# The first modulation vectors: five of eight weight pieces summed on TensorE instead of VectorE

## The reference

```python
ada = jax.nn.silu(c) @ w_ada[l] + b_ada[l]          # c: (1, 1024), w_ada[l]: (1024, 6144)
sh1, sc1, g1, sh2, sc2, g2 = [a[:, None, :] for a in jnp.split(ada, 6, axis=-1)]
h = x * (1.0 + sc1) + sh1
...
qa, ka, va, qb, kb, vb = jnp.split(h @ w_in, AB_SPLITS, axis=-1)
```

## Time and profile before

| | |
|---|---|
| median of three runs | 1322.96 us |
| the profiled execution | 1323.02 us, span 1321.2 us |
| TensorE busy | 1236.3 us (94%) |
| VectorE busy | 678.9 us (51%) |
| ScalarE busy | 512.3 us (39%) |
| DMA | 394.99 MB, mean 299 GB/s |
| TensorE busy in the first 20 us | 1.46 us |
| first matmul of weight unit 0 | 20.01 us |
| first matmul of weight unit 4 | 52.65 us |

### The profile page before, as it was taken

How to read it: one execution, slowest core, us unless ns; L and a number is a source line. 1 busy time by engine, 2 the same in 40 slices (tenths; PEclk the granted TensorE clock), 3 DMA queues, 4 the chain that set the end, 5 groups by cost and what they waited for, 6 DMA issues and landing times.

```text
span 1321.2 us, 16525 instructions
## 1 busy us (share of the span) xinstructions
PE 1236.3 (94%) x6620; PEld 856.5 (65%) x6620; DVE 678.9 (51%) x1178; ACT 512.3 (39%) x744; POOL 70.1 (5%) x107
## 2 busy tenths in 40 slices
PE   4898799999999999999999999999999999999977
PEld 2787577788778877788887887444444444544435
DVE  6678868698766777764558566111111111111145
ACT  2646464344464457443445275111111211112135
POOL 0101000000000000001000300000000000000021
PEclk9998899999999999999999999999999999999998
DMA  9988567998555535776555678999999999999960
GB/s 376 373 285 210 206 245 280 270 349 318 213 192 206 193 124 200 262 287 204 197 191 203 205 270 355 381 427 429 429 429 428 369 430 428 429 429 429 428 252 32
DMA packets 43689, 394.99 MB, mean 299 GB/s; under 512 B 5712, under 2 KB 6432, under 8 KB 9712
## 3 DMA queue, kind: packets, MB, share of 16 engines
q1 hardware_dynamic: 33424, 336.63, 64.6%
q0 software_dynamic: 9904, 57.34, 12.9%
q10 hardware_dynamic: 304, 0.23, 0.1%
HBM read 392.50 MB, written 2.46 MB: 299 GB/s over the span
## 4 chain that ended last, share of the span: by engine, by line
PE 60%; DMA 19%; DVE 12%; ACT 5%; issue 3%; SPq 1%; DVEq 0%; ACTq 0%
DMA slabs<-in_w 13%; PE psum L1220 13%; PE psum L676 9%; PE psum L683 9%; PE psum L679 9%; DMA w_raw<-in_units 5%; PE psum L1259 4%; DVE w_parts L1860 3%; ACT w_parts L1330 2%; PE psum L1167 2%; DVE aring L1843 2%; PE psum L949 1%; PE psum L729 1%; PE psum L961 1%; PE psum L1175 1%
## 5 line engine op out<-in xcount | busy, mean ns | idle before, releaser
L1860 DVE TENSOR_TENSOR w_parts<-w_raw,w_parts 128x2048 fp32r<-128x2048 f32 x110 | 251.4, 2289 | 121.4 <-ACT w_parts L1330 121.4
L1330 ACT ACTIVATE w_parts<-w_raw 128x2048 fp32r<-128x2048 f32 x110 | 209.6, 1911 | 121.9 <-DMA w_raw<-in_units 121.8
L1220 PE MATMUL psum<-slabs,arena 128*64 128x512 f32 x1024 | 224.3, 593 | 11.7 <-DMA slabs<-in_w 11.7
L676 PE MATMUL psum<-w_parts,h_parts 128*128 128x512 f32 x448 | 179.8, 401 | 17.3 <-DVE w_parts L1860 13.1
L679 PE MATMUL psum<-w_parts,h_parts 128*128 128x512 f32 x448 | 176.5, 394 | 0.0
L1220 PEld LDWEIGHTS psum<-slabs,arena 128*64 128x64 f32 x1024 | 72.8, 137 | 159.8 <-issue 141.0
L1330 ACT ACTIVATE arena<-psum 128x512 f32<-128x512 f32 (+1 forms) x59 | 33.3, 567 | 281.5 <-PE psum L1232 153.3
L683 PE MATMUL psum<-w_parts,h_parts 128*128 128x512 f32 x448 | 121.5, 394 | 0.0
L676 PEld LDWEIGHTS psum<-w_parts,h_parts 128*128 128x128 f32 x448 | 85.1, 190 | 39.9 <-DVE w_parts L1860 16.3
L683 PEld LDWEIGHTS psum<-w_parts,h_parts 128*128 128x128 f32 x448 | 85.2, 190 | 18.3
L1843 DVE CUSTOM_DVE_ANT_0 aring<-aring,cb 128x1024 f32<-128x1024 f32 x80 | 94.5, 1219 | 3.4 <-DMA aring<-in_ada 3.4
(11 more groups left out here) (306 smaller groups left out, 1769.1 us busy)
## 6 DMA issues: line engine op xcount, KB each, us to landing
slabs<-in_w SPq DMA_DIRECT2D x64, 2048.0 KB, 17.1
w_raw<-in_units SPq DMA_DIRECT2D x110, 1024.0 KB, 5.0
aring<-in_ada POOLq DMA_DIRECT2D x40, 1024.0 KB, 5.2
arena<-in_w SPq DMA_DIRECT2D x16, 2048.0 KB, 17.8
w_odd<-in_w SPq DMA_DIRECT2D x16, 2048.0 KB, 21.2
staged<-in_ada SPq DMA_DIRECT2D x8, 1024.0 KB, 18.3
ln_rows<-in_ln_rows POOLq DMA_DIRECT2D x4, 1024.0 KB, 7.4
slabs<-in_units SPq DMA_DIRECT2D x4, 1024.0 KB, 10.7
```

The lines of the kernel that those rows point to most:

```text
L676: mm(psum[:, bank, :], high(tile, tok), w_hi(k)[:, col:col + 512], start=first and bank not in begun, stop=False, skip_group_check=True)
L1220: ins = nc.tensor.matmul(psum[s * CAP:(s + 1) * CAP, w, :], xe_t[:, kt, s * CAP:(s + 1) * CAP], slab(w, s, b)[:, kt * FE:(kt + 1) * FE], s ...
L1330: return nc.scalar.activation(out_ap, in_ap, func, **kw)
L1860: v.tensor_tensor(w_lo(k), raw(k), w_hi(k).bitcast(F32), ALU.subtract).then_inc(w_split, 1)
```

## The change

Five of the first eight pieces, those at places 0, 1, 3, 5 and 7 (`BY_PE`), are now laid out with 128 inputs on the partitions. TensorE sums them: for each of two halves of 128 outputs, eight matmuls with a 128 x 128 block of the piece as the weights and one column of the activated `c` as the moving operand (`ada_piece`). VectorE only adds the bias to the sums in PSUM. Pieces 2, 4 and 6 stay on VectorE.

- `c` comes as 8 columns of `vec`, which is now the first transfer; ScalarE activates these 8 columns first. The copies `cb` are queued after unit 0 and activated after its high part.
- `x_first` comes in three transfers: tiles 0 and 1 ahead of piece 0, tiles 2 and 3 ahead of piece 2, tiles 4 to 7 ahead of piece 4.
- ScalarE does `first_h(p)` before the high part of unit p, VectorE does `first_low(p)` before the low part.
- TensorE does the 16 matmuls with the high weights of a unit first (L733 and L737 of the new file), for which it waits only for `w_hi_ready`, and the 8 with the low weights last (L744). Products of pieces 0 and 1 come first of all, that of piece 3 after unit 0, those of pieces 5 and 7 between the high and the low matmuls of units 1 and 2.
- GpSimd's first transfer waits for unit 3 instead of piece 7.

```diff
+BY_PE = (0, 1, 3, 5, 7)
...
+        def staged_count(n):
+            return 32 if n in (0, 2, 3, 5) else 16
+        def sums_of(n):
+            i = BY_PE.index(n)
+            return psum[:, 5 + i % 3, 2 * i:2 * i + 2]
...
             def stage(n):
-                sp.dma_start(staged[n][:], a["ada"][ADA_ORDER[n]]).then_inc(staged_in[n], 16)
+                src = a["ada_rows"][BY_PE.index(n)] if n in BY_PE else a["ada"][ADA_ORDER[n]]
+                sp.dma_start(staged[n][:], src).then_inc(staged_in[n], 16)
...
-            sp.dma_start(cb[:], a["c_rows"]).then_inc(silu_c, 16)
-            sp.dma_start(vec[:], a["vecs"]).then_inc(staged_in[0], 16)
+            sp.dma_start(vec[:], a["vecs"]).then_inc(silu_c, 16)
             for i in range(4):
+                if i == 1:
+                    sp.dma_start(cb[:], a["c_rows"]).then_inc(staged_in[2], 16)
+                if i < 3:
+                    tiles = slice(2 * i, 2 * i + 2 if i < 2 else KT)
+                    sp.dma_start(x_first[:, tiles, :], a["x_t"][:, tiles, :]).then_inc(staged_in[(0, 3, 5)[i]], 16)
                 stage(2 * i)
                 stage(2 * i + 1)
...
-            pool.wait_ge(staged_in[STAGED - 1], 16)
+            pool.wait_ge(w_loaded[3], 16)
...
+            def ada_piece(n):
+                pe.wait_ge(staged_in[n], staged_count(n))
+                pe.wait_ge(silu_c, 17)
+                for i in range(2):
+                    for kt in range(KT):
+                        ins = mm(sums_of(n)[:, i:i + 1], staged[n][:, kt * 256 + i * P:kt * 256 + (i + 1) * P],
+                                 V("c", kt), start=kt == 0, stop=kt == KT - 1)
+                ins.then_inc(ada_mm, 1)
+
+            def first_values(i, between=None):
+                k = V_AT + i
+                parts = [(2 * i + s, slice(1024 * s + 512 * c, 1024 * s + 512 * c + 512), c) for s in range(2) for c in range(2)]
+                pe.wait_ge(w_hi_ready, k + 1)
+                for t in range(TT):
...
+                if between is not None:
+                    ada_piece(between)
+                weights(k)
+                for t in range(TT):
...
+            ada_piece(0)
+            ada_piece(1)
...
-                    for i in range(4):
-                        ins = first_values(i, 0)
-                        if i == 3:
-                            ins.then_inc(v_half, 1)
-                        first_values(i, 1).then_inc(unit_done, 1)
+                    first_values(0)
+                    ada_piece(3)
+                    first_values(1, 5)
+                    first_values(2, 7)
+                    first_values(3)
...
             for p in range(4):
+                first_h(p)
                 split(p)
-                first_h(p)
+                if p == 0:
+                    act.wait_ge(staged_in[2], staged_count(2))
+                    A(cb[:], cb[:], ACT.Silu).then_inc(silu_c, 1)
...
+                if n in BY_PE:
+                    dve.wait_ge(ada_mm, BY_PE.index(n) + 1)
+                    v.tensor_tensor(ada_cols[:, col:col + 2], sums_of(n), V("b_ada", col, 2),
+                                    ALU.add).then_inc(ada_done, 1)
+                    return
...
             for p in range(4):
                 first_scale(p)
+                first_low(p)
                 split(p)
-                first_low(p)
```

## The result

| | before | changed |
|---|---|---|
| median, same chip | 1322.89 us (4 runs) | 1345.18 us (1341.72 to 1350.8, 4 runs) |
| ratio | | 1.017 (95% interval 1.0151 to 1.019) |
| span of the profiled execution | 1321.2 us | 1343.2 us |
| first matmul of unit 4 | 52.65 us | 75.17 us |
| first attention score on VectorE | 69.13 us | 91.67 us |

The change makes the kernel 22 us slower, and all of it is in place when unit 4 starts: 22.5 us there, 22.5 at the first score, 22.0 at the end.

A forecast was written before the change was run, and what follows sets the result against it. VectorE was taken to bound the first stage, ending at 52.65 us. Loop 9.75, half-clock start 2.9 and half clock behind waits 3.2 gave +15.9 us, 1338.9 us; bounds +7 to +23.8, own range 1330 to 1347.

The forecast's parts named there:

- The step that bounds: First stage, up to unit 4: its end at 52.65 us moves, and the shift carries to the end undiminished.
- rival 3: After the first stage: ScalarE and VectorE ahead at attention give back at most 3 us, 1335.9 us; chance 0.10.
- The loop: First stage: product, VectorE, ScalarE and high matmuls form a closed ring without transfers, 11.5 us a round against 8.0.
- passage: From the end of a product to the first high matmul: 4.2 us, four times, 16.8 us.
- Rival 1: First-stage products nearly free, below 1.36 us each, so the stage ends earlier: 1321.6 to 1322.7 us; chance 0.07.
- Loads: Front of the queue: pieces 0 and 1 land at 9.0 and 11.8 us, and no transfer binds.
- +2.9: Products 0 and 1 take the half-clock start: 2.9 us more, bounds 0 and 7.6.
- +3.2: Half clock behind the two long waits before units 0 and 1: 1.6 us each, bounds 0 and 6.4.
- the bound of 6.4: Upper bound in us for half clock behind waits before units 0 to 3: four falls.
- Rival 2: First stage: products do not lift the clock; products 0, 1, much of 3, 5, 7 and unit starts at half: 1352 us; chance 0.13.
- low end: Lower bound of the total: products of 2.9 us (four in series, -2.8) and no half clock, +7 us.
- Near nothing: Remaining edits, such as GpSimd's later transfer and row transfer: hidden by slack; `v_half` copy 0 to 0.5 us.

The follow-up runs named there:

- e1: Changed kernel with ScalarE doing the high part of unit p before `first_h(p)`, as before: ratio 1.012 to the kernel before, unit 4 at 68.25 us.
- e6: Changed kernel with 128 moving columns in all products, ScalarE's high part first, product 3 inside unit 0: ratio 1.0015 to the kernel before, unit 4 at 52.30 us.
- e5: Changed kernel with 128 moving columns in all five products: ratio 1.0151 to the kernel before, unit 4 at 70.93 us.
- e2: Changed kernel with the products of pieces 3, 5 and 7 one unit earlier on TensorE: ratio 1.0113 to the kernel before, unit 4 at 67.74 us.
- e3: Changed kernel with 37 unused 128-column transposes in TensorE's waits before units 0 to 3: ratio 1.0127 to the kernel before, median 1342.93 us.
- e11: Changed kernel with one-column products, ScalarE's high part first and product 3 inside unit 0: ratio 1.0109 to the kernel before, unit 4 at 65.70 us.
- e7: Kernel before, without products, with low-weight matmuls last and `first_low` ahead of VectorE's low part: ratio 1.0008, unit 4 at 54.08 us.
- e4: Changed kernel with 128 moving columns in the products of pieces 0 and 1 only: ratio 1.0121 to the kernel before, unit 4 at 68.95 us.
- e9: Changed kernel with products of 0, 1, 3 only, 128 columns, ScalarE's high part first, GpSimd's pieces 8 and 9 later: 1320.74 us, ratio 0.9971 to the kernel before.

## Why the prediction was right, and which term was too small

**The size.** The forecast was 15.9 us more, 22.3 were measured: inside the range of +7 to +23.8, but close to its top, which is the sum with both clock terms at their bounds. The mechanism held; the clock was priced too low.

**The step that bounds.** The stage up to unit 4 and nothing after it: right. The shift went from 22.5 us at unit 4 to 22.0 at the end; rival 3, a part given back later, didn't happen.

**The loop.** Right in each link. A passage took 4.1 us (37.6 to 41.71) for the 4.2 forecast, a product at full clock 3.5 us for 3.6, high matmuls at full clock 3.7. Rival 1 fell by the price of a product, 109 ns a record. e1 takes the high part out of the loop, e6 all of the cost.

**Loads.** Piece 0 was there at 8.16 us, forecast 9.0; no transfer bound anything later.

**The clock, mis-sized.** The terms "+2.9" and "+3.2" measured 6.7 and 7.7 us. The first two products took 13.75 us (8.16 to 21.91) where 7.0 would do. For the second term, the timeline of TensorE in the changed kernel:

```profile
25.97 2.08 PE L733 MATMUL psum<-w_parts,h_parts 128*128 128x512 f32 x4 [2.61 <-ACT w_parts L1367]
...
34.10 3.63 PE L720 MATMUL psum<-vec,staged 128*128 128x1 f32 x32
...
54.66 2.07 PE L733 MATMUL psum<-w_parts,h_parts 128*128 128x512 f32 x4 [1.53 <-ACT w_parts L1367]
...
60.31 3.63 PE L720 MATMUL psum<-vec,staged 128*128 128x1 f32 x32
...
67.93 1.20 PE L733 MATMUL psum<-w_parts,h_parts 128*128 128x512 f32 x4 [2.03 <-ACT w_parts L1367]
...
75.17 0.36 PE L764 MATMUL psum<-h_parts,w_parts 128*128 128x256 f32 x1
```

The matmuls of units 0 to 3 took 8.13 (25.97 to 34.10), 5.33, 5.65 (54.66 to 60.31) and 7.24 us (67.93 to 75.17), together 26.35, where 18.7 would do at full clock; those of units 0 and 3 hold the 8 low ones too. That is 2.5, 1.6, 1.9 and 1.6 us too long. The two terms are 8.3 us above the forecast. Less 0.8 for the earlier landing and about 0.8 in passages, products and matmuls, this is the 6.7 us between the forecast 68.5 and the measured 75.17 for unit 4.

Two steps failed in it. For the first term it is the assumption that products work on the clock like wider matmuls, taken from one run of 36 columns: the clock did not rise within them at all. For the second it is that only the two longest waits were charged, 1.6 us each. Half clock followed all four, of 2.61, 3.99, 1.53 and 2.03 us, and unit 0, before which the clock had never risen, lost 2.5. Single columns are not needed for that, since e5 with wide products loses 7.3 us in the same matmuls. The kernel before already had falls behind one wait of 2.28 us and none behind one of 2.26, so at this length the rows left it open, and the bound of 6.4 was the better guide.

Rival 2 had both products at half clock to their end and half clock in every unit: both came true, and with 9.75 + 7.6 + 6.4 us they are nearly the measured 22.5. It was wrong in its third term: the products between matmuls ran at full clock (3.5 us each), and only in other orders (e1, e2, e3, e11) did one or two of them run partly at half. So the outcome is the forecast's loop with two of rival 2's three terms. It lies in the range because the upper bound had priced both, not because the clock was foreseen.

One sum of the forecast was slightly wrong: its low end takes 0.7 us off four products in series, while its sum holds five, so it should be 3.5 us less and not 2.8. Nothing hung on it.

**The fall itself.** Two causes are shown apart. In e11 and e2 there are products of one column and no wait, and the clock falls. In e5 there are wide products and waits of 2.2 to 4 us, in e7 waits of 2.3 to 2.4 us and no products, and it falls as well. e6 has neither, no wait over 1.3 us after its first product, and the clock stays up. Which of several waits of 2.3 us brings a fall stays open. The Trainium skill, "TensorE: Matmul & The Clock Gate", section "HAM oscillation", describes short bursts of matmuls with longer waits between them, where every burst starts throttled. e5 agrees that waits bring the clock down, but there the bursts of about 9 us are longer than the waits of 2.2 to 4.0; e11's falls come without a wait, which the section does not speak of.

**Near nothing.** The low matmuls last and VectorE's order: e7 agrees, -0.06 to +0.21% in time.

## What to carry to other kernels

Before work is moved to an idle engine, draw the ring of waits: each step's release, and what stands ahead of it in its engine's queue. Here VectorE lost 12 us of work and the stage grew by 22, since each product stood behind the matmuls that needed the previous one. And look at what the moved work does to the clock. A record of one moving column took 109 ns at full clock, as long as one of 128 columns, and neither lifted the clock nor, in e11, held it up. If such a product must be on TensorE, widening it to 128 columns that nobody reads took no more time per record here, and made the stage of e6 13 us shorter than that of e11.

## What was not expected of the hardware

- With 128 moving columns instead of one, the 64 records of the first two products took 8.7 to 10.2 us (e4, e5, e6, e9) instead of 13.8, and the same record costs 109 ns in either form at full clock (3.48 and 3.49 us for 32).
- Two waits of 2.26 and 2.28 us ahead of the same kind of matmuls ended differently, one without and one with half clock behind it (before); so did those of 2.29 and 2.31 us in e7.
- Four runs of the changed kernel spread over 9 us (1341.72 to 1350.8) and four of the kernel before over 2. That this comes from clock falls is not shown: on another chip 23 runs of the kernel before spread over 10 us (1318.37 to 1328.73).
